# Bidirectional recurrence: both directions grown by VectorE in one instruction, levels seven slots apart, affine forms on ScalarE, memory weights normalised by VectorE

## What is computed

```python
# memory attention, every layer
logits = einsum('bshd,bmhd->bhsm', q, km)
probs = softmax(logits)
recalled = einsum('bhsm,bmhd->bshd', probs, vm)
# recurrence of layer 1, for both directions (the backward one on flipped tokens)
log_f = logaddexp(log(lb), log1p(-lb) + log_sigmoid(z))    # f = lb + (1 - lb) * sigmoid(z)
k = -expm1(log_f)                                          # k = (1 - lb) * sigmoid(-z)
attn[t, s] = sum_k q[t, k] * exp(cum[t, k] - cum[s, k]) * k[s, k]   for s <= t
o = attn @ v + (q * exp(cum)) @ state
# then RMS norm of the heads (6 of 128), times silu(g)
```

## Time and profile before

| | |
|---|---|
| median of 3 runs | 1368.01 us (1364.64 to 1371.36) |
| the profiled execution | 1369.13 us, its span 1367.3 us |
| mean granted TensorE clock | 0.986 |
| layer 1 from its input projection to the first norm | about 350 to 545 us |
| the same of layer 2 | about 748 to 848 us |
| layer 1's stretch, 195 us: busy | TensorE 186.4, VectorE 141.6, ScalarE 69.2, GpSimd 51.7 us |

### The profile page before, as it was taken

One profiled execution on the slowest core, in us unless ns is written; L12 is line 12 of the kernel. 1 busy time (PEld: TensorE's weight loads), 2 busy tenths in 40 slices (PEclk: granted clock), 3 DMA queues, 4 the chain that ended last, 5 costly groups with the idle time before them and its releaser, 6 DMA issues.

```text
span 1367.3 us, 23414 instructions
## 1 busy us (share of the span) xinstructions
PE 1317.2 (96%) x9366; PEld 1223.9 (90%) x9366; DVE 988.0 (72%) x1548; ACT 689.0 (50%) x1070; POOL 70.5 (5%) x92
## 2 busy tenths in 40 slices
PE   7999999999989999999999999999999998899997
PEld 6998999998988998999997898999998997899996
DVE  4665877778678867877778677777778666777777
ACT  4763555554732233655554634655553762555552
POOL 0001000000024421000000000000000000000000
PEclk9999999999999999999999999999999999999999
DMA  8643465554433233655553573755554542465551
GB/s 285 225 132 108 165 221 185 185 185 154 139 139 99 87 109 108 208 193 185 185 186 131 189 239 131 240 185 185 185 186 145 178 134 98 154 215 187 185 185 48
DMA packets 63400, 228.46 MB, mean 167 GB/s; under 512 B 7446, under 2 KB 9110, under 8 KB 62268
## 3 DMA queue, kind: packets, MB, share of 16 engines
q1 hardware_dynamic: 63292, 226.97, 49.2%
HBM read 225.88 MB, written 1.06 MB: 166 GB/s over the span
## 4 chain that ended last, share of the span: by engine, by line
PE 87%; DVE 7%; ACT 3%; issue 2%; POOL 1%; DMA 1%; SPq 0%; POOLq 0%; DVEq 0%; ACTq 0%
PE proj L579 18%; PE proj L580 17%; PE proj L581 17%; PE acc L606 8%; PE acc L608 7%; PE acc L607 7%; PE side L776 3%; DVE w_lo L970 2%; PE proj L591 1%; PE proj L593 1%; PE proj L595 1%; PE acc L677 1%; DVE y_tok L1129 1%; ACT w_hi L793 1%; PE side L720 1%
## 5 line engine op out<-in xcount | busy, mean ns | idle before, releaser
L579 PE MATMUL proj<-xT_hi,w_hi 128*128 128x256 f32 x2000 | 576.7, 288 | 10.6 <-DVE w_lo L970 6.4
L970 DVE TENSOR_TENSOR w_lo<-raw,w_hi 128x1024 fp32r<-128x1024 f32 x404 | 480.5, 1220 | 129.9 <-ACT w_hi L793 123.5
L580 PE MATMUL proj<-xT_lo,w_hi 128*128 128x256 f32 x2000 | 571.7, 286 | 0.0
L581 PE MATMUL proj<-xT_hi,w_lo 128*128 128x256 f32 x2000 | 571.4, 286 | 0.0
L793 ACT ACTIVATE w_hi<-raw 128x1024 fp32r<-128x1024 f32 x404 | 425.6, 1061 | 279.5 <-PE acc L608 132.1
L579 PEld LDWEIGHTS proj<-xT_hi,w_hi 128*128 128x128 f32 x2000 | 389.3, 195 | 19.3 <-DVE w_lo L970 12.4
L580 PEld LDWEIGHTS proj<-xT_lo,w_hi 128*128 128x128 f32 x2000 | 389.4, 195 | 1.5
L581 PEld LDWEIGHTS proj<-xT_hi,w_lo 128*128 128x128 f32 x2000 | 389.2, 195 | 0.0
L983 DVE SCALAR_TENSOR_TENSOR cv<-hid,fconv_w,cv 128x255 f32<-128x255 f32 x176 | 77.4, 481 | 138.1 <-ACT cv L833 138.1
L606 PE MATMUL acc<-w_hi,gT_hi 128*128 128x512 f32 x352 | 139.6, 396 | 3.1 <-DVE w_lo L970 3.1
L607 PE MATMUL acc<-w_lo,gT_hi 128*128 128x512 f32 x352 | 139.2, 395 | 0.0
(11 more groups left out here) (158 smaller groups left out, 1392.6 us busy)
## 6 DMA issues: line engine op xcount, KB each, us to landing
raw<-in_stream SPq DMA_DIRECT2D x404, 512.0 KB, 4.7
gains<-in_ln SPq DMA_DIRECT2D x8, 1024.0 KB, 8.4
bias<-bias_scratch SPq DMA_DIRECT2D x2, 1152.0 KB, 8.5
x_tok<-in_x SPq DMA_DIRECT2D x2, 512.0 KB, 5.0
y_tok<-in_mem SPq DMA_DIRECT2D x1, 1024.0 KB, 11.6
out<-x_tok SPq DMA_DIRECT2D x4, 256.0 KB, 2.0
masks_in<-in_masks_c SPq DMA_DIRECT2D x1, 512.0 KB, 7.7
fconv_w<-in_fconv SPq DMA_DIRECT2D x1, 264.0 KB, 7.7
```

The costliest lines, as they stand in the source:

```text
L579: pe.matmul(bank, w_hi[:, slot, at], a_hi(k, every), start=(k == 0), stop=False)
L580: pe.matmul(bank, w_hi[:, slot, at], a_lo(k, every), start=False, stop=False)
L581: last = pe.matmul(bank, w_lo[:, slot, at], a_hi(k, every), start=False, stop=(k == KT - 1))
L970: v.tensor_tensor(w_lo[:, u % SPLIT, :], raw[:, u % RAW, :], w_hi[:, u % SPLIT, :].bitcast(F32), ALU.subtract).then_inc(lo_ready, 1)
```

## The change

- The growth of both directions moves to VectorE, in one instruction for both: `qd`, `ke` and `tot` become one tensor each with the direction as an axis, and `block_parts` builds an access pattern that takes the right half of each block in each direction. Three instructions a growth on VectorE (keys, queries, totals), none on GpSimd; `bw_ready` goes.
- The affine forms of `FF` and `FB` move from VectorE to ScalarE, behind the sigmoids.
- The pairs start at slots 6, 13 and 20. `hpv`, `ms` and `scale` keep their slots.
- `xnorm` goes; `xprob` on VectorE makes the reciprocal and one product of 1024 columns. In layers 1 and 2 `xturn` and `xpv` move up by one slot, to 3 to 6.

```diff
@@ -99,8 +99,8 @@
...
-                  3: [it("xnorm", 0), it("xexp", 1), it("log", 0)], 4: [it("exp", 0), it("xprob", 1)],
-                  5: [it("xturn", 0), it("xnorm", 1), it("log", 1)], 6: [it("exp", 1), it("prob", 0)],
+                  3: [it("xexp", 1), it("log", 0)], 4: [it("exp", 0), it("xprob", 1)],
+                  5: [it("xturn", 0), it("log", 1)], 6: [it("exp", 1), it("prob", 0)],
...
             at = {0: [it("xlog", 0), it("xexp", 0), it("xlog", 1), it("xexp", 1)], 1: [it("xprob", 0), it("xprob", 1)],
-                  2: [it("xnorm", 0), it("xnorm", 1)], 4: [it("xturn", 0)],
-                  5: [it("xpv", 0)], 6: [it("xturn", 1)], 7: [it("xpv", 1)]}
+                  3: [it("xturn", 0)], 4: [it("xpv", 0)], 5: [it("xturn", 1)], 6: [it("xpv", 1)]}
...
             at = {0: [it("xlog", 0), it("xexp", 0), it("xlog", 1), it("xexp", 1)], 1: [it("xprob", 0), it("xprob", 1)],
-                  2: [it("xnorm", 0), it("xnorm", 1)], 4: [it("xturn", 0)],
-                  5: [it("xpv", 0)], 6: [it("xturn", 1)], 7: [it("xpv", 1)]}
-            for p, first in enumerate((6, 12, 18)):
+                  3: [it("xturn", 0)], 4: [it("xpv", 0)], 5: [it("xturn", 1)], 6: [it("xpv", 1)]}
+            for p, first in enumerate((6, 13, 20)):
                 for n in range(LEVELS + 1):
                     at.setdefault(first + n, []).append(it("level", p, n))
...
-        QD = [sb(f"qd{d}", [P, HEADS, SEQ]) for d in range(2)]
-        KE = [sb(f"ke{d}", [P, HEADS, SEQ]) for d in range(2)]
-        TOT = [sb(f"tot{d}", [P, HEADS * SEQ]) for d in range(2)]
+        qd = sb("qd", [P, 2, HEADS, SEQ])
+        ke = sb("ke", [P, 2, HEADS, SEQ])
+        tot = sb("tot", [P, 2, HEADS * SEQ])
+        QD, KE, TOT = [[t[:, d] for d in range(2)] for t in (qd, ke, tot)]
...
+        def block_parts(of, p, b, upper, count):
+            other = HEADS * SEQ
+            return bass.AP(tensor=of, offset=2 * p * SEQ + upper * b,
+                           ap=[[2 * other, P], [other + (1 - 2 * upper) * b, 2], [2 * b, SEQ // b],
+                               [1 if count else 0, b]])
...
                     pe.wait_ge(fw_ready[p], max(1, n))
-                    if n >= 2:
-                        pe.wait_ge(bw_ready[p], n - 1)
...
+                    d = 0 if role == "FF" else 1
+                    if index == 0:
+                        act.wait_ge(x_ready, x_count(2 * layer - 1, 1, 1))
+                    act.wait_ge(sig_ready, m + 1)
+                    for i in range(2):
+                        h, s = 2 * index + i, slice(i * SEQ, (i + 1) * SEQ)
+                        w = slice(d * HEADS + h, d * HEADS + h + 1)
+                        nc.scalar.activation(KE[d][:, h, :], sig[:, 0, s], ACT.Copy, scale=one_lb[:, w])
+                        last = nc.scalar.activation(TOT[d][:, h * SEQ:(h + 1) * SEQ], sig[:, 1, s], ACT.Identity,
+                                                    bias=lb[:, w], scale=one_lb[:, w])
+                    last.then_inc(sig_used, 1)
...
-                elif name == "xnorm":
-                    u = ordinal[pos]
-                    n = xprob_ord[u]
-                    act.wait_ge(xinv_ready, u + 1)
-                    for i in range(2):
-                        for t in range(TT):
-                            j = 2 * i + t
-                            last = nc.scalar.activation(prob[:, n % 2, i, t, :], ex[:, n % 2, i, t, :], ACT.Copy,
-                                                        scale=row_inv[:, n % 2, j:j + 1])
-                    last.then_inc(xprob_ready, 1)
...
-        def grow_blocks(eng, queue, link, ready, n, d, p):
-            b = 2 ** (n - 1)
-            before = n - d
-            if before > 0:
-                queue.wait_ge(ready, before)
-            nb = 2 * SEQ // (2 * b)
-            def blocks(flat):
-                return flat.rearrange("p (n two b) -> p n two b", two=2, b=b)
-            tot = blocks(TOT[d][:, p * 2 * SEQ:(p + 1) * 2 * SEQ])[:, :, :, 0:1]
-            qs = blocks(QD[d][:, 2 * p:2 * p + 2, :].rearrange("p h s -> p (h s)"))
-            ks = blocks(KE[d][:, 2 * p:2 * p + 2, :].rearrange("p h s -> p (h s)"))
-            qh, kh = 1 - d, d
-            eng.tensor_tensor(qs[:, :, qh, :], qs[:, :, qh, :], tot[:, :, 1 - qh, :].broadcast_to([P, nb, b]), ALU.mult)
-            link(eng.tensor_tensor(ks[:, :, kh, :], ks[:, :, kh, :], tot[:, :, 1 - kh, :].broadcast_to([P, nb, b]),
-                                   ALU.mult))
-            eng.tensor_tensor(tot[:, :, 0, :], tot[:, :, 0, :], tot[:, :, 1, :], ALU.mult).then_inc(ready, 1)
...
-                elif role in ("FF", "FB"):
-                    d = 0 if role == "FF" else 1
-                    if index == 0:
-                        dve.wait_ge(x_ready, x_count(2 * layer - 1, 1, 1))
-                    dve.wait_ge(sig_ready, sig_ord[c] + 1)
-                    for i in range(2):
-                        h, s = 2 * index + i, slice(i * SEQ, (i + 1) * SEQ)
-                        w = slice(d * HEADS + h, d * HEADS + h + 1)
-                        v.tensor_scalar(KE[d][:, h, :], sig[:, 0, s], one_lb[:, w], None, ALU.mult)
-                        last = v.tensor_scalar(TOT[d][:, h * SEQ:(h + 1) * SEQ], sig[:, 1, s], one_lb[:, w], lb[:, w],
-                                               ALU.mult, ALU.add)
-                    last.then_inc(sig_used, 1)
...
+            def grow_blocks(p, n):
+                b = 2 ** (n - 1)
+                def parts(of, upper, count):
+                    return block_parts(of, p, b, upper, count)
+                dve.wait_ge(fw_ready[p], n)
+                v.tensor_tensor(parts(ke, 0, b), parts(ke, 0, b), parts(tot, 1, 0), ALU.mult)
+                link(v.tensor_tensor(parts(qd, 1, b), parts(qd, 1, b), parts(tot, 0, 0), ALU.mult))
+                whole = bass.AP(tensor=tot, offset=2 * p * SEQ, ap=[[2 * HEADS * SEQ, P], [HEADS * SEQ, 2], [2 * b, SEQ // b]])
+                lower = bass.AP(tensor=tot, offset=2 * p * SEQ + b, ap=[[2 * HEADS * SEQ, P], [HEADS * SEQ, 2], [2 * b, SEQ // b]])
+                v.tensor_tensor(whole, whole, lower, ALU.mult).then_inc(fw_ready[p], 1)
...
                     if name == "xprob":
-                        v.reciprocal(row_inv[:, s, :], row_sum[:, s, :]).then_inc(xinv_ready, 1)
+                        link(v.reciprocal(row_inv[:, s, :], row_sum[:, s, :]))
+                        v.tensor_tensor(prob[:, s].rearrange("p i t s -> p (i t) s"),
+                                        ex[:, s].rearrange("p i t s -> p (i t) s"),
+                                        row_inv[:, s, :].rearrange("p (j one) -> p j one", one=1).broadcast_to([P, 4, SEQ]),
+                                        ALU.mult).then_inc(xprob_ready, 1)
...
                     if 1 <= n < LEVELS:
-                        grow_blocks(v, dve, link, fw_ready[p], n, 0, p)
+                        grow_blocks(p, n)
...
-                elif name == "level" and 1 <= item[3] < LEVELS:
-                    p, n = item[2], item[3]
-                    pool.wait_ge(fw_ready[p], 1)
-                    pool.wait_ge(level_done[p], n + 1)
-                    grow_blocks(nc.gpsimd, pool, link, bw_ready[p], n, 1, p)
```

More of the change, by code:

```diff
@@ L375, in trunk_kernel @@
         logits_done, max_ready, exp_ready, prob_ready = sem("logits_done"), sem("max_ready"), sem("exp_ready"), sem("prob_ready")
-        xinv_ready, xprob_ready = sem("xinv_ready"), sem("xprob_ready")
+        xprob_ready = sem("xprob_ready")
         prob_turned, probT_ready = sem("prob_turned"), sem("probT_ready")
@@ L387, in trunk_kernel @@
         fw_ready = [sem(f"fw_ready{p}") for p in range(PAIRS)]
-        bw_ready = [sem(f"bw_ready{p}") for p in range(PAIRS)]
         lam_dots, lam_exps, lb_diff, lb_exp = sem("lam_dots"), sem("lam_exps"), sem("lb_diff"), sem("lb_exp")
```

## The result

| | before | after |
|---|---|---|
| median | 1368.01 us (7 runs) | 1374.19 us (7 runs, 1372.96 to 1378.09) |
| ratio to before | 1 | 1.0060, 95% interval 1.0044 to 1.0076 |
| the profiled execution | 1369.13 us | 1372.96 us, its span 1371.1 |
| mean granted TensorE clock | 0.986 | 0.983 |

The changed kernel is slower: by 0.6% by the ratio, which is some 8 us, by 6.2 us by the medians and by 3.8 us by the two profiled executions. The prediction had 1376.0, a range of 1365 to 1383, and slower (0.47) just ahead of the same (0.46).

What follows compares the result with a forecast made beforehand. TensorE, busy 96% of the span, bounds the kernel. Levels +9.9, early -3.2 and layer 2 +1.2 sum to +7.9 us on the profiled 1369.1, so 1377.0, or 1376 against the median; range 1365 to 1383 (8 in 10).

Steps and rivals of the forecast that it cites:

- The levels: Layer 1's recurrence: new bank waits 6.6 + 1.4, 0.3 behind query posts, clock 6.9 + 0.6, less 5.9: +9.9 us.
- the 0.15 twice behind the query posts: Recurrence, slots 11 and 17: growth starts 1.5 us late and ends some 0.15 after the half, twice.
- the old 5.9: Levels of layer 1 before: 4.3 us of waits and 1.6 of clock, all taken as gone.
- The early part: Layer 1's memory attention: new wait 2.7 and clock 1.5, less 7.4 us of old waits and clock: -3.2 us.
- the 1.5 that was taken: Clock lost behind the new wait before `xpv` 0 in layer 1: 1.5 us, from a span of 0 to 3.4.
- Layer 2: Memory attention: new wait 2.4 us before `xturn` 0, clock 0.8, less 2.0 of old waits: +1.2 us.
- the 0.8 for it: Clock lost behind layer 2's new wait: 0.8 us, from a span of 0 to 1.6.
- Layers 0 and 3, and growth: Weights' product of 1.2 us hidden in VectorE's slack, cost 0; growth of 1.4 to 2.0 us under the 2.9 half.
- rival (d): Growth: strided products of 512 columns run slower than dense, a growth passes 2.9 us; 6 us more, 1382 us; chance 0.03.
- (a): TensorE: the waits come but the clock stays full, so bank waits cost only themselves; 1369 us; chance 0.35.
- (b): Faster: ScalarE's chain to `xpv` 0 short enough, early repair complete, clock full; -7.4 + 2.4 - 1.0 = -6, 1362 us; chance 0.08.
- (c): More clock lost: a slot's low stretch reaches into the level next to it each time; 1384 us; chance 0.07.

Runs made afterwards that it cites:

- the first experiment: The changed kernel with only the pairs' starts back at slots 6, 12 and 18: 1362.48 us, 0.9958 to the kernel before.
- the second experiment: The changed kernel with its new starts, bank chosen by level number modulo 2 and `ms` of pair 1 on bank 0: 1361.87 us, 0.9956 to the kernel before.
- the ninth: The changed kernel with 17 unused matmuls of 256 columns ahead of each of the three long bank waits: 1370.76 us, 1.0034 to the kernel before.
- The eighth experiment: The changed kernel with only layer 2's memory attention moved, transposes at slots 4 and 7, products at 5 and 8: 1371.85 us, 1.0039 to the kernel before.
- seven: The kernel before with only the growth changed, both directions by VectorE in one instruction, none on GpSimd: 1362.89 us, 0.9974 to the kernel before.
- ten: The changed kernel with all slots as before (starts 6, 12, 18; memory attention of layers 1 and 2 at 4 to 7): 1359.63 us, 0.9953 to the kernel before.
- experiments three: The kernel before with only the pairs' starts changed to slots 6, 13 and 20: 1384.03 us, 1.0119 to the kernel before.
- four: The changed kernel with the memory attention of layer 1 back at slots 4 to 7: 1372.60 us, 1.0032 to the kernel before.
- five: The changed kernel with only the affine forms back on VectorE: 1371.16 us, 1.0035 to the kernel before.

## Why the prediction was right

**The levels** (predicted +9.9). By the starts of the mixer's levels and of the FFN, the part of layer 1 behind the memory attention grew by 8.1 us. Every bank wait that was worked out came, at its place and size: 2.24, 2.23 and 2.32 for 2.2 three times, 0.69 twice for 0.7, and for the 0.15 twice behind the query posts 0.5 in two pieces. The clock was the term with an error. The half behind the first and the third wait took 4.45 us each, 1.55 more than usual; the second had a stretch twice as long, in which level (2,0) and its half lost 2.7:

```profile
462.86 2.08 PE L773 MATMUL side<-q,ksum 128*128 128x128 f32 x8 [2.23 <-DVE dg L1216]
464.59 0.56 PE L597 MATMUL proj<-w_hi,xT_hi 128*128 128x256 f32 x1
...
469.36 1.05 PE L785 MATMUL side<-qd,ke 128*128 128x128 f32 x8
```

That is 5.8 in place of 6.9, and the short waits cost no clock in place of 0.6. Waits 6.8 + 1.4 + 0.5, clock 5.8, less the old 5.9: 8.6, of the 8.1 found. The first two experiments show the cause, the ninth that a share of it is clock.

The Trainium skill, "PSUM — Partial Sum Buffer", § PSUM bank collisions raise a hardware error, has PSUM guarded by bank (and within it by 32 partitions), not by address; it has no price for it. The kernel's semaphores guard whole banks, and the second experiment shows the price of that: with other banks, and nothing else changed, the waits of 2.2, 2.2, 2.3 and 0.7 twice are gone. No run here leaves the guard out, so the rule itself is not tested.

**The early part** (predicted -3.2). Measured -2.9: level (0,1) starts at 390.62 against 390.24, but at full clock, and the next level at 395.27 against 398.16. The wait is 3.1 where 2.7 was worked out. ScalarE's chain, step by step, is where this comes from. The groups of after's affine forms (columns as in the earlier trace rows) and the chain's end in its timeline:

```profile
L860 ACT ACTIVATE tot<-sig,lb,one_lb 128x256 f32<-128x256 f32 x12 | 7.0, 586 | 0.0
L859 ACT ACTIVATE ke<-sig,one_lb 128x256 f32<-128x256 f32 x12 | 6.0, 501 | 0.3
```
```profile
373.37 0.51 ACT L859 ACTIVATE ke<-sig,one_lb 128x256 f32<-128x256 f32 x1
373.78 0.58 ACT L860 ACTIVATE tot<-sig,lb,one_lb 128x256 f32<-128x256 f32 x1
374.27 0.49 ACT L859 ACTIVATE ke<-sig,one_lb 128x256 f32<-128x256 f32 x1
374.67 0.58 ACT L860 ACTIVATE tot<-sig,lb,one_lb 128x256 f32<-128x256 f32 x1
375.16 1.05 ACT L917 ACTIVATE xprobT<-side 128x512 f32<-128x512 f32 x2
```

The sum took the distance of the old copies, 0.41 us, for all four. The two with one operand keep it (373.37 to 373.78), the two with scale and bias take 0.49 and 586 instead of 501 ns. Four of them lie in the chain, 0.3 of the 0.4 us of error. The rest is small: a gap of 0.1 ahead of each group of copies, a little at the hand-over to TensorE, and TensorE itself asking 0.3 later. Here the better source was the Trainium skill, "ScalarE: Activation LUTs", § What ACT_TABLE_LOAD costs, with about 93 ns for each pointer operand. The trace agrees with 586 - 501 = 85. The sum of -2.8 by it was nearer than the prediction's. The clock behind that wait lost about as much as the 1.5 that was taken: `xpv` 0 at 376.36 took 1.84 us where `xpv` 1 takes 1.09, with the half behind it slow at first.

**Layer 2** (predicted +1.2). Measured +0.1. The new wait of 2.4 came to the tenth, behind the product, but the clock stayed full, so the 0.8 for it fell away, and 2.4 - 2.0 is nearly all that is left. The eighth experiment takes the wait out and is 2.9 us below after by the ratios, 2.3 by the medians, which is about the 2.4, though not clear of the noise. Other executions with the same wait did lose clock (below), so the 0.8 was not unreasonable as a mean, only wrong for this trace.

**Layers 0 and 3, and growth.** The product is 1225 ns there (predicted 1.2 us) and hidden; both stretches are within 0.1 us of before. A growth's products are 692 and 686 ns for 512 columns (predicted 0.69), so rival (d) falls.

**The sum.** Levels 8.1, early -2.9, layer 2 +0.1 are +5.3. The profiles differ by only 3.8, because before's execution had a low stretch at the first norm of layer 1 that after's had not, 1.5 us:

```profile
550.00:552.00 2.00, 2.00 (x13) 2.00 (x12) 1.94 (x3) 2.00 (x4) 0.00 (x0) 0.60 0.70 240
```

It may belong to the starts. Of the twelve executions traced, the four with the old starts (before, experiments one, seven and ten) all have this stretch, at 536 to 554, and the eight with the new starts have none, though the waits at that norm are the same. The prediction had no such term, and why the starts should matter there is open. The medians differ by 6.2. The predicted +7.9 was too high by the 1.7 of clock in the levels and the 1.1 in layer 2, less 0.3 early. Against the profiled 1372.96 the 1377.0 of the sum is 4.0 too high, these 2.5 and the 1.5 at the norm. That 1376 lies within 2 us of the median, 1374.19, is in part luck: the median stands above the profiled execution by 1.2 for after and below it by 1.1 for before.

**The rivals.** (a), a clock that stays full, is out: it is low behind all three long waits in every execution traced with them (after, and experiments three, four, five and eight), and the filler of the ninth takes all three low stretches away. (b) needed a chain to `xpv` 0 that is 2.7 us shorter; it was 0.4 longer. Its price of -6 had a last term of -1.0, for layer 2, where the prediction's own least was +0.4; with that it would have been -4.6, and nothing else hangs on it. (c), a longer stretch, happened once in three in after's trace, in two of three in those of experiments four and eight, in one of three in that of three, and never in that of five. It is no case of its own but the upper end of the forecast.

The diff as a whole, taken apart: growth -0.26% (seven), the affine forms and the product together -0.2% more in the old slots (ten against seven, whose intervals just overlap, so not shown), early memory attention no gain, the new starts +1.0%.

## What to carry to other kernels

When items of a software pipeline are moved against each other, write down for each slot which buffers its items take: two that follow each other in one bank expose the reader's whole queue, which with its clock here cost some 14 us in 1370 and was undone by another bank index. Ordering the reader so that what frees the bank comes ahead of work nobody is waiting for is the other remedy that the timeline suggests; it was not tried. Here, with TensorE 96% busy, a bank wait of 2.2 us cost 3.8 to 4.9 in after's trace, since the clock behind it was at half speed.

## What the runs showed of the hardware

**The clock's answer to a wait is not the same every time.** The same wait of 2.4 us before layer 2's first transposes left the clock full in after (the window at 776 above), but in the first experiment, whose list is the same there, it fell:

```profile
761.91 1.34 PE L695 MATMUL side<-ident,prob 128*128 128x128 f32 x7 [2.39 <-DVE prob L1161]
```
```profile
762.00:764.00 2.00, 2.00 (x12) 2.00 (x13) 2.00 (x2) 1.10 (x3) 0.00 (x0) 0.60 0.04 8
764.00:766.00 2.00, 2.00 (x12) 2.00 (x12) 1.97 (x4) 1.04 (x2) 0.00 (x0) 0.55 0.19 47
```

Of the six executions traced with this wait, five have the low stretch. Likewise the wait of 3.1 us before `xpv` 0 cost nothing in the first experiment, some 1.5 us in after and about twice that in the second (low from 374 to 381). Why one and not the other is open. The price of a low stretch, though, is not spread evenly: added up over the 2 us windows of the twelve traces, those in the mixers of layers 1 and 2 and at their norms each lose either 1.7 us or 3.4. All this makes the clock a term with a spread: kernels with the same waits differ by several us, and before itself ran between 1363.7 and 1371.7 on one chip, at mean clocks of 0.990 and 0.984.

**Work kept the clock full though nobody used it.** In the ninth experiment's trace 2.3 us of matmuls whose result nobody reads kept it at 1.00 at three places where the bare waits had lowered it in all five executions traced with them.

**Two engines on the same kind of product slow each other.** A key product of 256 columns took 822 ns on VectorE with GpSimd at work beside it; alone, 512 columns take 692. GpSimd's three products of a growth took 898, 894 and 450 ns on average in before's trace. So one engine doing twice the work was no slower than two: a growth of both directions lasts 1.5 us in after's timeline above.
